# Token order of a hybrid decoder step: residue, block and run, with moved norms and mean matmuls on column halves

## What is computed, cut to what matters

```python
x = x + 0.5 * swiglu(rmsnorm(x, norm_ffn1), w_gate, w_up, w_down)          # inner width 2816
h = rmsnorm(x, norm_mix)
z = h @ w_in            # pool input u (512) | 3 groups x (q, k, v) x 4 heads x 64 | two gates (1024 each)
# branch A: trailing means over 2, 4, 8, 16 tokens of four 128-channel groups, minus the token, a linear map
# branch B: per group a dilated causal window: (128, 1), (512, 4), (2048, 16); merged by softmax denominators
x = x + (sigmoid(gate_pool) * A + sigmoid(gate_attn) * B) @ w_o
x = x + 0.5 * swiglu(rmsnorm(x, norm_ffn2), ...)
y = rmsnorm(x, norm_final)      # also returned: the last pool inputs, the last rotated keys and the values
```

## Time and profile before

| | before |
|---|---|
| time, median of 3 runs | 2924.14 us (2923.12 to 2925.61) |
| time of the profiled execution | 2923.13 us |
| its span on the slowest core (core 4) | 2921.9 us |
| spans of all cores | 2911.1 to 2921.9 us |
| PE busy | 2815.1 us (96%) |
| VectorE, ScalarE, GpSimd busy | 1038.7, 755.7, 331.0 us |
| mean granted TensorE clock, core 4 | 0.987 |

### The profile page before, as it was taken

The page is one execution under the profiler, slowest core; times in us unless marked ns, Lnnn a source line. Parts: engine busy times, 40 slices in busy tenths (PEclk is TensorE's granted clock), DMA queues, the critical chain, the costliest instruction groups (busy, mean ns, idle before and its releaser), DMA issues.

```text
span 2921.9 us, 47174 instructions; the slowest of 8 cores (2911.1 to 2921.9 us)
## 1 busy us (share of the span) xinstructions
PE 2815.1 (96%) x16993; PEld 1350.6 (46%) x17306; DVE 1038.7 (36%) x1704; ACT 755.7 (26%) x1340; POOL 331.0 (11%) x448
## 2 busy tenths in 40 slices
PE   7999988999999999999999999999999999999997
PEld 2444544444444455444444445444444445544443
DVE  3212753421241166442142128542124216644112
ACT  2111233312121124421122113432112112442111
POOL 1000620000000044000000007000000004400000
PEclk8999998999999999999999999999999999999999
DMA  9666765765353334343343424344224223433221
GB/s 212 146 150 134 192 150 139 182 171 139 107 173 107 110 125 153 109 146 127 103 152 110 138 80 149 125 131 148 83 75 165 71 89 119 144 118 114 73 75 70
DMA packets 97089, 372.58 MB, mean 128 GB/s; under 512 B 12472, under 2 KB 14168, under 8 KB 93660
## 3 DMA queue, kind: packets, MB, share of 16 engines
q1 hardware_dynamic: 75760, 270.81, 27.7%
q0 software_dynamic: 17648, 86.94, 13.9%
q10 hardware_dynamic: 3456, 11.80, 1.0%
HBM read 342.66 MB, written 99.03 MB: 151 GB/s over the span
## 4 chain that ended last, share of the span: by engine, by line
PE 89%; DVE 4%; issue 3%; DMA 2%; ACT 1%; ACTq 0%; SPq 0%; DVEq 0%; POOL 0%; POOLq 0%
PE ps L198 89%; DMA sb_xT<-x 1%; DVE sb_hT L507 1%; DMA sb_uexs<-spoolT 1%; DVE sb_ystg L507 1%; DMA kp<-sb_kf 1%; DVE sb_rtmp L579 1%; DVE sb_pbuf L765 0%; DVE sb_V L214 0%; DVE sb_kf L579 0%; DVE sb_kf L917 0%; ACT sb_pbuf L761 0%; ACT sb_V L213 0%; DMA sb_kT<-kcs 0%; DVE sb_mergedT L919 0%
## 5 line engine op out<-in xcount | busy, mean ns | idle before, releaser
L198 PE MATMUL ps<-sb_hT,sb_w 128*128 128x512 bf16 x7461 | 1685.2, 381 | 31.6 <-issue 6.3
L198 PEld LDWEIGHTS ps<-sb_hT,sb_w 128*128 128x128 bf16 x7680 | 740.6, 98 | 920.2 <-issue 61.0
L525 ACT ACTIVATE sb_stmp<-ps 128x512 f32<-128x512 f32 x352 | 209.8, 597 | 920.5 <-PE ps L198 871.2
L198 PE MATMUL ps<-sb_actTB,sb_w 128*128 128x512 bf16 x1371 | 316.6, 379 | 1.8
L198 PE MATMUL ps<-sb_actTA,sb_w 128*128 128x512 bf16 x1382 | 316.2, 379 | 1.8 <-DVE sb_actTs L526 0.2
L468 ACT ACTIVATE sb_sq<-sb_xT 128x512 bf16<-128x512 f32 x224 | 139.4, 630 | 666.7 <-DVE sb_xT L570 467.3
L526 DVE TENSOR_TENSOR sb_actTB<-sb_stmp,ps 128x512 bf16<-128x512 f32 x176 | 120.9, 687 | 485.8 <-PE ps L198 472.3
L526 DVE TENSOR_TENSOR sb_actTA<-sb_stmp,ps 128x512 bf16<-128x512 f32 x176 | 119.9, 686 | 421.1 <-PE ps L198 417.1
L570 DVE SCALAR_TENSOR_TENSOR sb_xT<-ps,sb_xT 128x512 f32<-128x512 f32 x128 | 87.8, 690 | 434.3 <-PE ps L198 421.2
L198 PEld LDWEIGHTS ps<-sb_actTA,sb_w 128*128 128x128 bf16 x1408 | 136.9, 98 | 163.7 <-issue 0.2
L198 PEld LDWEIGHTS ps<-sb_actTB,sb_w 128*128 128x128 bf16 x1408 | 136.7, 98 | 163.7
(11 more groups left out here) (134 smaller groups left out, 1528.5 us busy)
## 6 DMA issues: line engine op xcount, KB each, us to landing
sb_w<-wscr SPq DMA_DIRECT2D x341, 512.0 KB, 4.0
sb_w<-wch POOLq DMA_DIRECT2D x83, 512.0 KB, 8.3
wscr<-sb_w SPq DMA_DIRECT2D x83, 512.0 KB, 4.5
sb_w<-wscr SPq DMA_DIRECT2D x52, 384.0 KB, 3.5
kvs<-c POOLq DMA_DIRECT2D x32, 511.8 KB, 5.0
y<-sb_ystg POOLq DMA_DIRECT2D x7, 2048.0 KB, 12.1
sb_xT<-x SPq DMA_DIRECT2D x8, 1024.0 KB, 11.9
sb_xT<-x SPq DMA_DIRECT2D x4, 2048.0 KB, 10.8
```

Of the source, the lines that this page charges most:

```text
L198: self.pe.op(lambda: self.nc.tensor.matmul(out, lhsT, rhs, start=start, stop=stop, **kw), reads=reads, writes=writes, inc=inc)
L525: act.op(lambda: nc.scalar.activation(out=st[:, 0:n], in_=ps[bg][:, 0:n], func=AF.Silu), reads=[psr[bg]], writes=st.r)
```

## The change

Runs now stand in their natural order, so a block of group 0 is 16 stretches of 8 columns. Keys and values of group 0 are kept block by block. For that `proj` copies `sb_hT` into block order, into a new buffer that lies on `kf` and `vtok`, with four copies on ScalarE and four on VectorE for each tile, after the u groups. The rotated keys of group 0 are written in block order. Six places of the schedule are edited: the first loads, `nfin`, the sample rows' pooling (its VectorE part, `sample_mid`, is split from its matmuls, `sample_mid2`), the buffer of the tanh results, A's norm inside the gates of B, and the last store. Some norms (`half`) run their mean matmuls in pairs on two halves of the array's columns.

```diff
+        hblk = [layout(i * XB + 4 * T * 4, [("hblk%d" % i, [128, 8, T], BF16, 8)])["hblk%d" % i] for i in range(3)]
...
-        for i in range(2):
-            sp.dma(xb[0][:, 4 * i:4 * i + 4, :], ...ds_xh[i]...)
+        for i in range(4):
+            sp.dma(xb[0][:, 2 * i:2 * i + 2, :], ...ds_xh[i]...)
...
+        pool.wait_tok((ds_xh[1].sem, ds_xh[1].total))
         w_issue(2)
-        pool.wait_tok((ds_xh[1].sem, ds_xh[1].total))
+        pool.wait_tok((ds_xh[3].sem, ds_xh[3].total))
         w_issue(4)
...
             def flush(self):
+                while self.half and len(self.pend) > 1:
+                    pair, self.pend = self.pend[:2], self.pend[2:]
+                    for k, sq in enumerate(pair):
+                        i = self.n_mm
+                        self.n_mm += 1
+                        K.mm(ps[self.b][64 * k:64 * k + 64, 0:self.seg.n], meanm[:, 0:64], sq[:, 0:self.seg.n], i < 2, i > 5,
+                             reads=pair[0].r + pair[1].r + meanm.r if k == 0 else (), ...)
...
             def head(self):
+                if self.half:
+                    lo, hi = slice(0, 64), slice(64, 128)
+                    act.op(lambda: nc.scalar.copy(out=seg.rstd[lo, 0:n], in_=ps[b][hi, 0:n]), ...)
+                    dve.op(lambda: nc.vector.tensor_tensor(out=seg.rstd[lo, 0:n], in0=seg.rstd[lo, 0:n], in1=ps[b][lo, 0:n], op=ALU.add), ...)
+                    act.op(...Ln on rstd[lo]...)
+                    for o in (hi, lo):
+                        act.op(...Exp of rstd[lo] into rstd[o]...)
+                    K.give(b)
+                    return
...
-                for (d0, d1, s0, s1) in ((4, 32, 0, 28), (1, 4, 28, 31)):
-                    e.op(lambda: ne.tensor_copy(out=ev[:, 0:w - 1, d0:d1], in_=ev[:, NR:NR + w - 1, s0:s1]), ...)
+                e.op(lambda: ne.tensor_copy(out=ev[:, 0:w - 1, 1:NI], in_=ev[:, NR:NR + w - 1, 0:NI - 1]), ...)
...
+            hb0 = hblk[K.free]
+            def copies(cs):
+                for c in cs:
+                    K.copy(dve if c % 2 else act, blk(hb0[:, c, :]), nat(seg.hT[:, c, :]), [seg.hT.r[c]], [hb0.r[c]])
...
             if i == 1:
                 pool_mm()
+            K.claim(hb0)
+            copies(range(8))
...
-                hs = (lambda kc, q: seg.hT[:, kc, q:T:4]) if g == 0 else (lambda kc, q: seg.hT[:, kc, q * 128:(q + 1) * 128])
+                hv = hb0 if g == 0 else seg.hT
+                hs = lambda kc, q: hv[:, kc, q * 128:(q + 1) * 128]
...
+                    if g == 0 and half == 1:
+                        K.claim(kf, vtok)
...
-            def col(g, u, tt=None):
-                return slice(u, T, 4) if g == 0 else slice(u * 128, (u + 1) * 128)
+            def col(ap, g, u):
+                return ap.rearrange("p (r u c) -> p u r c" if g == 0 else "p (u r c) -> p u r c", u=4, c=8)[:, u]
...
-                        if mid is not None:
-                            mid()
-                            mid = None
+                        if mid and n == T:
+                            mid.pop(0)()
...
         def attn_s():
-            sample_mid()
+            sample_mid2()
...
+            if with_s:
+                sample_mid()
             merge(main_(), 52.0, fill, 21.5 + (24.0 if with_s else 0.0))
...
-                nA.all({0: 12, 4: 6})
+                nA.all({0: 8, 2: 2, 4: 2, 6: 2})
...
-                nB = Norm(B)
+                nB = Norm(B, True)
...
-                    hooks[("mid", 0)] = nfin
+                    first = hooks[("A", 0)]
+                    hooks[("A", 0)] = lambda nfin=nfin: (nfin(), first())
...
-            gt = mx["kf"]
+            gt = Part(mx["rtmp"][:, 0:2, :], mx["rtmp"].r[0:2])
...
-            def mid():
+            def midA():
                 A.norm.flush()
-                A.norm.finish(2)
+                A.norm.head()
+            mids = [midA] + [lambda i=i: A.norm.scale(2, range(2 * i, 2 * i + 2)) for i in range(4)]
...
-            A.norm, B.norm = Norm(A), Norm(B)
+            A.norm, B.norm = Norm(A, True), Norm(B, nextp)      # second FFN
...
-                n2 = Norm(seg(0, xb[K.free]))
+                n2 = Norm(seg(0, xb[K.free]), True)
...
+                if not nextp:
+                    B.norm.head()
+                    for i in range(4):
+                        B.norm.scale(3, range(2 * i, 2 * i + 2), ystg[1])
+                        (sp, act)[i % 2].dma(y_d[s, tB, :, 2 * i:2 * i + 2, :], ystg[1][:, 2 * i:2 * i + 2, :], ds_yl[i], ...)
+                    return
...
 def _run(c):
-    return 8 * (c % 4) + c // 4
+    return c
```

More of the change, by code:

```diff
@@ L338, in build @@
         ds_x2 = [DmaSem(K, "ds_x2%d" % i) for i in range(2)]
+        ds_yl = [DmaSem(K, "ds_yl%d" % i) for i in range(4)]
         ds_rope = DmaSem(K, "ds_rope")
@@ L464, in add @@
                 ring_ = sqb if n == T else sqs
+                assert any(id(x) not in sq_live for x in ring_)
+                while id(ring_[sq_i[0] % len(ring_)]) in sq_live:
+                    sq_i[0] += 1
                 sq = ring_[sq_i[0] % len(ring_)]
                 sq_i[0] += 1
+                sq_live.add(id(sq))
                 if (eng or act) is act:
@@ L475, in flush @@
             def flush(self):
+                while self.half and len(self.pend) > 1:
[4 more added lines that the diff above has]
+                        K.mm(ps[self.b][64 * k:64 * k + 64, 0:self.seg.n], meanm[:, 0:64], sq[:, 0:self.seg.n], i < 2, i > 5,
+                             reads=pair[0].r + pair[1].r + meanm.r if k == 0 else (), writes=[psr[self.b]] if k == 0 else (), inc=(k == 1))
+                        sq_live.discard(id(sq))
+                    EngW.commit((pe.sem, pe.cnt), pair[0].r + pair[1].r, [psr[self.b]])
+                if self.half:
+                    return
                 for sq in self.pend:
@@ L496, in head @@
                 seg, n, b = self.seg, self.seg.n, self.b
+                if self.half:
+                    lo, hi = slice(0, 64), slice(64, 128)
+                    act.op(lambda: nc.scalar.copy(out=seg.rstd[lo, 0:n], in_=ps[b][hi, 0:n]), reads=[psr[b]], writes=seg.rstd.r)
+                    dve.op(lambda: nc.vector.tensor_tensor(out=seg.rstd[lo, 0:n], in0=seg.rstd[lo, 0:n], in1=ps[b][lo, 0:n], op=ALU.add),
+                           reads=[psr[b]] + seg.rstd.r, writes=seg.rstd.r)
+                    act.op(lambda: nc.scalar.activation(out=seg.rstd[lo, 0:n], in_=seg.rstd[lo, 0:n], func=AF.Ln, bias=EPS, scale=1.0),
+                           reads=seg.rstd.r, writes=seg.rstd.r)
+                    for o in (hi, lo):
+                        act.op(lambda: nc.scalar.activation(out=seg.rstd[o, 0:n], in_=seg.rstd[lo, 0:n], func=AF.Exp, scale=-0.5), reads=seg.rstd.r,
+                               writes=seg.rstd.r)
+                    K.give(b)
+                    return
                 act.op(lambda: nc.scalar.activation(out=seg.rstd[:, 0:n], in_=ps[b][:, 0:n], func=AF.Ln, bias=EPS, scale=1.0),
@@ L683, in qk @@
                                                           in_=kf[:, :, :].rearrange("p a (r c) -> p a r c", c=NI)), reads=kf.r, writes=kres)
+                        elif g == 0:
+                            for ab in range(2):
+                                act.op(lambda: nc.scalar.copy(out=blk(kT0[:, t % 3, ab, :]), in_=nat(kf[:, ab, :])), reads=kf.r, writes=kres)
                         else:
@@ L1219, in build, with nfin @@
             nfin = None
-            def nfin(B=B, gB=gB, s=s, tB=tB):
+            def nfin(B=B, gB=gB, s=s, tB=tB, nextp=nextp):
                 for sg in gB:
@@ L1235, in build @@
         issue_copy(1000)
-        for d in [ds_misc] + ds_so + [st_sems[i][k] for i in range(2) for k in out_kinds]:
+        for d in [ds_misc] + ds_so + ds_yl + [st_sems[i][k] for i in range(2) for k in out_kinds]:
             if d.total > 0:
```

41 lines of the change are left out of this document (25 added, 16 removed).

## The result

The changed kernel takes 2940.77 us (median of 6 runs) against 2923.63 us for the kernel before beside it: a ratio of 1.0057, 95% interval 1.0044 to 1.0071. It is slower, and the time lies above the range of 2888 to 2937. Some executions ran with the cores of one die at a lower granted clock; they are left out of every ratio here, and where few others remained the single times are given.

A forecast was written before the change was run, and what follows sets the result against it. PE, busy for 96% of the span, was taken as the bound. Gains of -58 us against costs of +48.7 gave -9.3 on 2923.1; with the median 1.0 above, 2915 us, range 2888 to 2937.

The forecast's parts named there:

- Both new stalls: PE waits 8.5 us for a square behind the moved norm, and 5.0 us a pair for tile A's block copies.
- the forecast's 23.7: First FFN of pairs 1 to 3: the moved final norm delays B's squares on VectorE, +23.7 us with clock loss.
- The wait at tanh: Gates: tanh results leave `kf`, so PE's 8.2 us wait behind the `kp` store goes; with clock -9.9 us.
- The last store's -3: End of the kernel: the last store leaves in quarters instead of one 2 MB store, -3 us.
- -2.6: Mean matmuls paired on column halves in both FFNs: 11.2 us of columns saved less 8.6 for mode changes, net -2.6 us.
- the +2 for the next B's head: First FFN: the longer norm head delays B's scales, 0.7 us for each of three, +2 us.
- Group 0's -25.5: Attention of group 0: score, value and denominator matmuls reach group 1's price, 28 us less 2.5 for new waits.
- The block copies, +21 and +2: Projections: PE waits for tile A's copies behind B's norm on VectorE, +21 us (10 to 28); tile B's wait for stores, +2.
- the -2.5: Start: the first weights no longer compete with the first half of x, -2.5 us (0 to 5).
- Rival 1: One new stall, moved norm or block copies, is hidden: 2893 us, chance 0.15; both hidden: 2870, chance 0.05.
- rivals 2 and 3: Group 0: value and denominator matmuls keep their price, 2928 us, chance 0.12; stretches of 8 gain nothing, 2940, chance 0.08.
- rival 4: Tile B's block copies do wait for A's `kp` and `vp` stores, 4 us a tile: 2931 us, chance 0.14.

The follow-up runs named there:

- the combined version: The changed kernel with the final norm back, all means full, tile A's block copies on ScalarE in the first FFN, and late k casts: 0.9853 of the kernel before, 2879.35 us.

## Why the prediction was wrong

**Right.** Both new stalls (that of the copies in size partly by luck), group 0's step prices, and the norm's move: with full means the first FFN grew by 18.5 us (20.5 by the median of the cores), and the forecast's 23.7 less its three half heads (copy, add, one Exp: 1.84 each) is 18.2. The wait at tanh went (gates of A -15.0 in pair 0), and A's norm in the gates with its neighbours gave 8.7 (6.5 forecast). The last store's -3 comes out once the halves are gone: with full means 14.1 us follow the last down matmul, against 16.9 before.

**The steps that failed**, by their share of the 25.8 us between 2915 and 2940.8:

- "GpSimd has one carry copy fewer per group, on an engine busy for 11%", costed at nothing: +10. The engine's mean busy share hid that in the projections it is busy for half of the time, next to VectorE sums that it can block, and that a shift of less than 1 us decides whether it does. The step was undone twice, in the change and in the combined version, and gave 10 us both times.
- The halves. "-2.6", the +2 for the next B's head and the 5.5 inside the norm's move make +4.9; they cost 16, and 22 with the norm back in its place. The saving was 0.8 in the down matmuls, not 2.6. The head is paid in the first FFN twice (the old B's and the next B's), with a lower granted clock behind the stall, and in the last pair, where the mean matmul waits 3.37 us for a square against 1.26: "in the second FFN that lies under at least 2.4 us of down matmuls" did not hold there. The forecast's list of PE's waits in the kernel before had left out those for squares, 10.9 us in five waits on ScalarE and 4.7 in three on VectorE: the longer head came into a chain on which PE waited already. How the 16 splits between the longer head, the pairs that wait for the later square, and the clock was not tried.
- Group 0's -25.5, half of it. With the old carries and no copies, the stages from values to gates are 2.8 us shorter than before (6.3 by the median of the cores), where the steps alone are worth 12.7. PE is faster there and waits for VectorE. Under the gates of A VectorE has time (22.63 of 45.80 us busy in pair 1), and the order gave its 11 (forecast 12.7).
- The block copies, +21 and +2: 12 by the last run without them. This error went the other way, for the same reason: the stall at the copies and the waits at the first masks are one backlog of VectorE, paid where PE first meets it.

In this order +10, +11 (16 less 4.9), +11 (9.9 in the projections, 1.7 under the gates) and -11 (12 less 23): 21 of the 26. Each is a difference of runs that do not simply add, so the sum is rough. The rest is the start, where the -2.5 did not show (PE waits 4.8 us for weights that now begin behind half of x), and the gates of pair 0. Rival 1 fell with the two stalls, rivals 2 and 3 with the step prices; of rival 4, waits of tile B's copies for a store, the waits of PE, VectorE and ScalarE in the change show nothing.

That VectorE, slowed by GpSimd, sets the projection stages was shown by the run without the adds. How the 12 of the copies splits between their own time on VectorE (0.29 us for most, up to 1.49), what they delay, and the clock was not tried.

## What to carry to other kernels

Work out VectorE's and GpSimd's load for the stretch that is changed, not for the span: at 36% and 11% overall, they were busy for 78 and 52 of 101 us in the projections of pair 1, and GpSimd was what slowed VectorE. Two edits on one chain of an in-order engine are priced together or not at all: undone singly they gave 10 and 13 us, together 32, and a stall that is merely moved comes back at the next place where the engines meet. A faster TensorE step is worth its columns only where the engine that feeds it has time; here it became worth 19.5 us after the casts in front of the exps, the copies and the collision were out of the way.

## What the runs showed of the hardware

Two sums of SBUF operands on VectorE took 1.29 us when they began before GpSimd's add and 5.19 behind adds of 2.2 and 2.3 us, by the rows each until the add in progress had ended; products with one operand in PSUM took 0.62 either way. A copy on VectorE with one SBUF input took 0.29 us in the median and 1.35 beside a GpSimd instruction of 1.45. 16 stretches of 8 columns ran at the price of contiguous ones in scores, values and denominators, where a step of 4 cost 0.48 us more in 16 score matmuls.
